# Five small moves of work at stage ends in a two-block transformer kernel: down-projection inputs, selected rows, a key product's bank, low parts

## The reference

```python
q = (xc @ wq).reshape(PEER_CHUNK, PEER_HEADS, 2, half)
sc = jnp.einsum('chpd,hpnd->chpn', q, sub_keys)
s1, i1 = lax.top_k(sc[:, :, 0], PEER_TOPK)          # 16 of 128 in each half
s2, i2 = lax.top_k(sc[:, :, 1], PEER_TOPK)
# the best 16 of the 16 x 16 sums, softmax g over them, expert index = i1 * 128 + i2
a = gelu(einsum('chkd,cd->chk', u[eidx], xc), exact)
out = einsum('chk,chkd->cd', g * a, v[eidx])
```

```python
hn = rmsnorm(h, norm_ffn_pre)
g, up = jnp.split(hn @ w_gate_up, 2, axis=-1)       # 2816 each
h = h + rmsnorm((jax.nn.silu(g) * up) @ w_down, norm_ffn_post)
```

## Time and profile before

| what | us |
|---|---|
| median of 3 runs | 2596.41 |
| lowest and highest | 2592.62, 2598.65 |
| profiled execution, its own time | 2602.34 |
| span of the profiled execution | 2600.5 |
| TensorE busy | 2461.7 (95%) |
| VectorE busy | 1758.9 (68%) |
| ScalarE busy | 1339.2 (51%) |
| GpSimd busy | 700.6 (27%) |

### The profile page before, as it was taken

How to read it: one execution, slowest core, us unless ns; L and a number is a source line. 1 busy time by engine, 2 the same in 40 slices (tenths; PEclk the granted TensorE clock), 3 DMA queues, 4 the chain that set the end, 5 groups by cost and what they waited for, 6 DMA issues and landing times. The chain is left out here.

```text
span 2600.5 us, 57098 instructions
## 1 busy us (share of the span) xinstructions
PE 2461.7 (95%) x16535; PEld 2249.7 (87%) x16535; DVE 1758.9 (68%) x3854; ACT 1339.2 (51%) x2350; POOL 700.6 (27%) x533
## 2 busy tenths in 40 slices
PE   7889999999999999998899999999999989888998
PEld 6789999999888887888899999988888886778986
DVE  5637777887677777655777788777777665514346
ACT  3434555776555555443455577655555434323443
POOL 5655444000000000656444200000000150324665
PEclk9989999999999999999999999999999999888999
DMA  6234666445566666433466544456666544322543
GB/s 245 70 128 158 216 227 222 161 158 179 187 242 242 242 242 229 171 112 132 160 222 217 216 146 163 176 208 242 241 242 241 184 155 149 111 74 106 179 171 143
DMA packets 97759, 475.23 MB, mean 183 GB/s; under 512 B 11776, under 2 KB 13312, under 8 KB 50432
## 3 DMA queue, kind: packets, MB, share of 16 engines
q1 hardware_dynamic: 97104, 472.91, 50.6%
q10 hardware_dynamic: 560, 1.19, 0.1%
HBM read 438.41 MB, written 35.65 MB: 182 GB/s over the span
## 5 line engine op out<-in xcount | busy, mean ns | idle before, releaser
L1233 ACT ACTIVATE wh<-ring 128x512 fp32r<-128x512 f32 x1428 | 881.9, 627 | 618.6 <-ACTq L1232 616.0
L1758 DVE TENSOR_TENSOR wl<-ring,wh 128x512 fp32r<-128x512 f32 x961 | 683.7, 716 | 276.3 <-DVEq L1757 258.7
L485 POOL TENSOR_TENSOR wl<-ring,wh 128x512 fp32r<-128x512 f32 x295 | 389.7, 1341 | 1536.7 <-POOLq L484 1533.3
L972 PE MATMUL PS<-xh,wh 128*128 128x256 f32 x2048 | 593.9, 290 | 9.1 <-PEq L968 7.8
L972 PE MATMUL PS<-xl,wh 128*128 128x256 f32 x2048 | 579.2, 283 | 0.0
L972 PE MATMUL PS<-xh,wl 128*128 128x256 f32 x2048 | 579.2, 283 | 0.0
L798 PE MATMUL PS<-wh,xh 128*128 128x512 f32 x1112 | 435.1, 391 | 7.3 <-PEq L795 7.3
L798 PE MATMUL PS<-wl,xh 128*128 128x512 f32 x1112 | 433.4, 390 | 0.0
L798 PE MATMUL PS<-wh,xl 128*128 128x512 f32 x1112 | 433.3, 390 | 0.0
L972 PEld LDWEIGHTS PS<-xh,wh 128*128 128x128 f32 x2048 | 391.9, 191 | 16.2 <-issue 15.4
L972 PEld LDWEIGHTS PS<-xl,wh 128*128 128x128 f32 x2048 | 392.4, 192 | 0.0
(11 more groups left out here) (292 smaller groups left out, 3750.9 us busy)
## 6 DMA issues: line engine op xcount, KB each, us to landing
ring<-in_peer_u SPq DMA_DIRECT2D x128, 1024.0 KB, 4.8
ring<-in_peer_v SPq DMA_DIRECT2D x128, 1024.0 KB, 4.8
acts<-stg SPq DMA_DIRECT2D x124, 256.0 KB, 2.0
gains<-acts SPq DMA_DIRECT2D x124, 256.0 KB, 4.8
ring<-in_w_in SPq DMA_DIRECT2D x24, 1024.0 KB, 4.9
ring<-in_w_gate_up SPq DMA_DIRECT2D x22, 1024.0 KB, 4.7
ring<-in_peer_wq SPq DMA_DIRECT2D x16, 1024.0 KB, 4.8
ring<-in_w_down SPq DMA_DIRECT2D x11, 1024.0 KB, 4.8
```

Source lines behind the costliest of these rows:

```text
L485: part = pool.tensor_tensor(wl[:, q, :], ring[:, s, q * QW:(q + 1) * QW], wh[:, q, :].bitcast(F32), SUB)
L972: last = pe.matmul(PS[:, 2 * j, 0:S], w[:, q, k * P:(k + 1) * P], x[:, at, :], start=at + i == 0, stop=at + i == 9)
L1233: act.activation(wh[:, q, :], ring[:, s, q * QW:(q + 1) * QW], ACT.Copy).then_inc(high_ready[q], 1)
L1758: part = dve.tensor_tensor(wl[:, q, :], ring[:, s, q * QW:(q + 1) * QW], wh[:, q, :].bitcast(F32), SUB)
```

## The change

- The last two gate-up chunks are taken out of the loops of TensorE and DVE. In the last one, TensorE signals a new semaphore `x_used` with the first product of quarter 1. DVE waits for it and stages both halves of the first down chunk before it takes the last gate-up result. ACT casts quarters 0 to 2 of the first down chunk before the last silu and quarter 3 after it.
- The transposes of the selected rows stand before chunk 37 of the experts, not behind it. DVE copies them before the low part of quarter 3 of chunk 38.
- The last key product of a layer writes bank 4 (slot 2) and waits for that slot.
- In `residual_rows` the low part of the next chunk's quarter 3 stands between the two sums of squares.

```diff
-            def chunks(n, first, f, full, scales=None):
+            def chunks(n, first, f, full, scales=None, x_done=None):
...
-                with pe.Fori(0, n // 2 - 1):
+                with pe.Fori(0, n // 2 - (2 if x_done else 1)):
                     for s in (0, 1):
                         f(s, full)
+                if x_done:
+                    f(0, full)
+                    f(1, full, x_done)
...
+                                if x_done and q == 1 and b + k + i == 0:
+                                    last.then_inc(x_done, 1)
...
-                def key_scores(c, s):
-
-                    pe.wait_ge(slot_free[1], 1)
-                    pe.sem_inc(slot_free[1], -1)
+                def key_scores(c, s, slot=1):
+
+                    pe.wait_ge(slot_free[slot], 1)
+                    pe.sem_inc(slot_free[slot], -1)
...
-                key_scores(N_WQ - 1, 1)
+                key_scores(N_WQ - 1, 1, 2)
...
-                with pe.Fori(0, N_GATE):
+                with pe.Fori(0, N_GATE - 1):
                     experts()
...
                                [(ps2(2 + t)[:, i * P:(i + 1) * P], sel[:, i, t, :]) for i in range(3)])
+                experts()
...
-            chunks(NFB, first_cols, chunk_by_cols, dve_full, row_scales)
+            chunks(NFB, first_cols, chunk_by_cols, dve_full, row_scales, x_used)
...
+                if next_first:
+                    for q in range(3):
+                        high(n % 2, q)
                 if result:
                     result(n - 1, (n - 1) % 2)
+                if next_first:
+                    high(n % 2, 3)
...
                 def scores_out(c, s):
 
-                    act.wait_ge(act_full[1], 1)
-                    act.sem_inc(act_full[1], -1)
+                    slot = 2 if isinstance(c, int) and c == N_WQ - 1 else 1
+                    act.wait_ge(act_full[slot], 1)
+                    act.sem_inc(act_full[slot], -1)
...
-            high_parts(NFB, squares_to_xT, silu, peel=1)
-            high_parts(NFB // 2)
+            high_parts(NFB, squares_to_xT, silu, peel=1, next_first=True)
+            high_parts(NFB // 2, begun=True)
...
                     s, cols = c % 2, slice(CW * c, CW * (c + 1))
-                    if c:
-                        low(s, 3)
                     take_rows(s)
...
                     for t in range(TT):
                         sum_of_squares(o_all[:, t, cols], t, sums4[:, t, c:c + 1])
+                        if t == 0 and c < 3:
+                            low(1 - s, 3)
...
-                for q in range(4):
+                for q in range(3):
                     low(0, q, 2)
                 for t in range(TT):
                     dve.wait_ge(dve_full[2 + t], 1)
...
+                low(0, 3, 2)
                 own(dve.engine_nop())
...
+            with dve.Fori(1, NFB // 2 - 1) as i:
+                for s in (0, 1):
+                    low(s, 3)
+                    gate_up(s, 2 * i + s)
+            low(0, 3)
+            gate_up(0, NFB - 2)
+            low(1, 3)
+            dve.wait_ge(x_used, 1)
+            dve.sem_inc(x_used, -1)
             for j in range(2):
                 stage_down(0, j)
+            gate_up(1, NFB - 1)
+
             low(0, 3)
```

More of the change, by code:

```diff
@@ L207, in build @@
         acc_seen = sem("acc_seen")
+        x_used = sem("x_used")
         dve_lows_done = sem("dve_lows_done")
@@ L763, in rows_by_chunk, with chunk_by_cols @@
                     last.then_inc(full[s], 1)
-            def chunk_by_cols(s, full):
+            def chunk_by_cols(s, full, x_done=None):
                 pe.wait_ge(slot_free[s], 1)
@@ L936, in _ @@
                 pe.wait_ge(keys_in, 16)
-                def key_scores(c, s):
-                    pe.wait_ge(slot_free[1], 1)
-                    pe.sem_inc(slot_free[1], -1)
+                def key_scores(c, s, slot=1):
+                    pe.wait_ge(slot_free[slot], 1)
+                    pe.sem_inc(slot_free[slot], -1)
                     for t in range(TT):
                         for p in range(2):
-                            last = pe.matmul(PS[:, 2, (2 * t + p) * NK:(2 * t + p + 1) * NK],
+                            last = pe.matmul(PS[:, 2 * slot, (2 * t + p) * NK:(2 * t + p + 1) * NK],
                                              qTc[:, s, p, t * P:(t + 1) * P],
                                              peer_k[:, c, p * NK:(p + 1) * NK], start=True, stop=True)
-                    last.then_inc(act_full[1], 1)
+                    last.then_inc(act_full[slot], 1)
                 first_cols(act_full)
@@ L1235, in high_parts @@
             def high_parts(n, between=None, result=None, peel=0, late=None, following=False,
-                           mid=None, begun=False):
+                           mid=None, begun=False, next_first=False):
                 if not begun:
@@ L1403, in scores_out @@
                 def scores_out(c, s):
-                    act.wait_ge(act_full[1], 1)
-                    act.sem_inc(act_full[1], -1)
+                    slot = 2 if isinstance(c, int) and c == N_WQ - 1 else 1
+                    act.wait_ge(act_full[slot], 1)
+                    act.sem_inc(act_full[slot], -1)
                     act.wait_ge(scores_used, 1)
                     act.sem_inc(scores_used, -1)
-                    act.activation(scc[s][:, :, :], PS[:, 2, :].rearrange("p (a n) -> p a n", a=4),
+                    act.activation(scc[s][:, :, :], PS[:, 2 * slot, :].rearrange("p (a n) -> p a n", a=4),
                                    ACT.Copy).then_inc(act_own, 1)
@@ L1412, in scores_out @@
                     act.sem_inc(act_own, -1)
-                    act.sem_inc(slot_free[1], 1)
+                    act.sem_inc(slot_free[slot], 1)
                     act.sem_inc(scores_ready, 1)
@@ L2522, in gate_up @@
                 dve.sem_inc(act_used, 1)
[L2524 to L2530, removed]
             def stage_down(c, j):
@@ L2537, in stage_down @@
                                   SUB).then_inc(wst_ready[j], 1)
+            gate_up(0, 0)
+            low(1, 3)
+            gate_up(1, 1)
+            with dve.Fori(1, NFB // 2 - 1) as i:
[4 more added lines that the diff above has]
+            gate_up(0, NFB - 2)
+            low(1, 3)
+            dve.wait_ge(x_used, 1)
+            dve.sem_inc(x_used, -1)
             for j in range(2):
                 stage_down(0, j)
+            gate_up(1, NFB - 1)
             low(0, 3)
```

## The result

The changed kernel takes 2583.18 us in the median of five runs (2578.61 to 2585.24); the kernel before took 2596.41 us beside it (2592.62 to 2604.5). The ratio is 0.994, with a 95% interval of 0.9925 to 0.9956. The forecast was 2584 us. The profiled execution took 2583.18 us, with a span of 2581.4 and a mean granted clock of 0.982 (before 2602.34, 2600.5 and 0.975). The profiles are 19.1 us apart and the medians 13.2, and the interval of the ratio reaches from 11.4 to 19.5 us. Of the profiles' 19.1 us, 4.1 lie in a place that nobody touched: it is told at the end.

What follows compares the result with a forecast made beforehand. TensorE, busy 95% of 2600.5 us, was taken to bound the kernel, so only its waits and the slow clock behind them could be won. 6.5 + 4.1 + 1.6 + 0.3 = 12.5 us off the median 2596.41 gave about 2584, range 2577 to 2592.

Steps and rivals of the forecast that it cites:

- down parts early: End of gate-up: 5.15 us wait and 1.9 us of clock go, 0.55 comes back; 6.5 us, between 5.0 and 7.0.
- low parts between sums: Output stages: waits of 2.28 and 0.53 us go, with 1.3 of slow clock; 4.1 us, between 2.0 and 4.6.
- transposes sooner: Before the one-hots: they start sooner, 0.8 us a layer, TensorE still waiting 2 us; 1.6 us, between 0.4 and 2.2.
- own bank: Last key product: its 2.67 us wait goes, but TensorE waits later for DVE; 0.3 us for both layers.
- middle case for DVE: Early down staging: first cast and subtraction go through, POOL holds the second pair, TensorE waits 0.35 us; 6.5 us gained.
- giving back: Down stage: 0.55 us returned, 0.35 for a late fourth low part and 0.2 for the third chunk's late ring half.
- Rival (a): Key product: DVE is no barrier, all 5.3 us come in place of 0.3; 2573 to 2580 us, chance 0.12.
- (b): Routing loops: the first layer takes on the second's waits, 6.1 us against 0.3, costing 5.8; 2590 us, chance 0.13.
- (c): Routing loops: a 1.7 us wait more in each of 16 turns, so slower; 2611 us, chance 0.04.
- sign of trouble: Routing loops: the prediction is wrong if waits in the two together change by more than 5 us.
- (d): Down stage: staging held four times and ring late, only half of 6.5 us won; 2587 us, chance 0.08.
- (e): All edited places: the change doesn't remove what it aims at, no measurable change; 2594 us, chance 0.06.

Runs made afterwards that it cites:

- stage_early: The changed kernel, but ACT casts all four quarters of the first down chunk after the last silu, as before; 2584.21 us, ratio 0.9943.
- cast_early: The changed kernel, but DVE stages the first down inputs after the last gate-up result, as before; 2586.57 us, ratio 0.9947.
- scores_first: The changed kernel, with ACT copying the seventh pair's scores out before the four casts of the first expert chunk; 2581.01 us, ratio 0.994.
- onehots_first: The changed kernel, with the first one-hot group built before the low part of chunk 38's fourth quarter; 2578.7 us, ratio 0.9924.
- both_first: The changed kernel with the edits of scores_first and onehots_first together; 2582.71 us, ratio 0.9932.
- copies_first: onehots_first, with DVE's two copies of the selected rows also ahead of the low parts of quarters 1 and 2; 2580.17 us, ratio 0.9921.
- row_only: The kernel before with only the selected rows transposed one chunk sooner; 2596.08 us, ratio 0.9988.
- low_only: The kernel before with only the low part moved between the two sums of squares; 2590.93 us, ratio 0.9966.
- key_only: The kernel before with only the last key product in its own bank; 2598.38 us, ratio 1.0002.
- down_only: The kernel before with only the down-stage part of the change; 2595.87 us, ratio 0.9978.
- after_again: The changed kernel unaltered, run again beside its variants; 2582.13 us, ratio 0.994.

## Why the prediction was right

| term | predicted | in the trace | run again |
|---|---|---|---|
| down parts early | 6.5 (5.0 to 7.0) | 5.4; alone 4.8 | 5.3 |
| low parts between sums | 4.1 (2.0 to 4.6) | 5.3 to 5.7; alone 5.3 | 5.3 |
| transposes sooner | 1.6 (0.4 to 2.2) | 2.0 | 0.5 |
| own bank | 0.3 (0 to 0.35 per layer) | 0.7 | 0.7 |
| sum | 12.5 | 13.4 to 13.8 | 11.8 |
| medians | 12.4 | 13.2 | |
| ratio as a time | | 15.6 (11.4 to 19.5) | 15.6 (11.4 to 19.5) |

**Down: the mechanism right, the term too large.** The first wait, the steps after it and the request of the third chunk (2509.06; 2522.7 less the 13.4 gained earlier is 2509.3) behaved as worked out. ACT's and POOL's early parts and DVE's staging are both needed, which stage_early and cast_early show. The middle case for DVE came true: first pair free, second held. The step that failed is the giving back. The sum took off 0.35 us for a late fourth low part and 0.2 for the third chunk's ring half, 0.55 in all; the waits behind the first product grew by 1.25. The two named are small or absent here (0.19 and 0.28 us at the second and third chunk), but a wait of 1.25 us stands in the fourth, where DVE's staging for it and POOL's low parts start within 0.3 us of each other. The same kernel run again has it (1.2), and scores_first, onehots_first, both_first and copies_first have 1.2, 1.2, 1.2 and 1.5. A kernel with the down part alone has one of 1.4, but ahead of the second chunk, also behind a cast and a subtraction of DVE that were held beside POOL's low parts. Of the two with half of the part, stage_early has 0.6 in the fourth chunk and cast_early 0.5 and 0.6 in the fifth and sixth, and the kernels without the part (before, row_only, low_only, key_only) have none over 0.35 behind the first wait. So it belongs to the early start. That the DVE operations beside POOL's are its cause is read from their rows; no kernel moved them apart. I had followed the change only as far as the third chunk. The clock gave 1.5 us instead of 1.9, since the first down chunk takes 5.85 us without its waits and not 5.55.

This agrees with the rule of the Trainium skill, page "SBUF — State Buffer", section "Who interferes with whom", that such operations of VectorE and GpSimd hold each other for a whole instruction and that the first to issue goes ahead: 0.42 us against 1.29 for one subtraction, 0.69 against 1.33 and 1.69 for one low part. The rule leaves it to the order of issue, and that changed from one execution to the next (the second cast above, 0.29 and 1.40).

**Low parts: the mechanism right, the term too small.** The second stage gave 4.0 us where 2.28 + 1.3 = 3.6 were expected, since the clock gave back some 1.5 to 1.7 instead of 1.3. The first stage was priced at its one wait of 0.53; it gave 1.3 or a little more, in steps of 0.7, 0.3 and 0.4 at waits of 0.53, 0.10 and 0.19. The last two are small waits at other quarters of that stage which the row I chose did not show. The one of 0.19 stands in row_only, key_only and down_only too and belongs to the edit; the one of 0.10 is absent in them, so that step is variation, and some 1.1 us are the edit's.

**Transposes: right up to the first one-hot product, and then left open.** The wait fell by 0.5 us, to 2.32 instead of the 2.0 expected, but the transposes also filled a wait ahead of them, and both together gave 1.0 us per layer instead of 0.8. This much recurs in both layers of all six traces with this part and a wait of 2.3 us. The prediction put the clock behind the wait that stays at nothing, and this was right in only one of six traces for the first layer: in the other five it took 1.55 us back. In the second layer the traces with this part gain 1.0 or 2.5 us, but key_only and low_only gain 1.6 without it and down_only loses 1.2. What this part is worth in a median stays open: the two layers gave 2.0 us in one execution of the changed kernel and 0.5 in the next, and row_only's interval reaches from -0.3 to 6.2.

**Own bank: right in kind.** TensorE waits later instead, 0.83 + 1.09 = 1.9 us where 2.5 were named. The low part of the fourth quarter took 0.69 instead of 1.03 us, and the quarter starts 0.34 us sooner, which is the upper end of what was given for a layer, and it came in both layers. Rival (a), which had 5.3 us here, is excluded by key_only (0.7 us in its trace) and scores_first.

**The routing loops, rivals (b) and (c).** TensorE's waits in the expert chunks of the first layer (245 to 470) and of the second (1262 to 1480), in this order for before, changed, down_only and low_only:

```profile
PE PS L972 <- PEq L968: 1.1, 4, 0.3
...
PE PS L972 <- PEq L968: 6.4, 11, 1.7
```

```profile
PE PS L978 <- PEq L974: 1.8, 5, 0.5
...
PE PS L978 <- PEq L974: 2.9, 6, 1.4
```

```profile
PE PS L978 <- PEq L974: 3.1, 11, 0.4
...
PE PS L978 <- PEq L974: 3.3, 6, 1.7
```

```profile
PE PS L972 <- PEq L968: 2.1, 7, 0.5
...
PE PS L972 <- PEq L968: 1.0, 3, 0.5
```

down_only and low_only run the program of before up to the end of the second layer, and yet their second layer waits 3.1 and 5.4 us less and their first 2.0 and 1.0 more. The difference between the layers that I read into rival (b) is variation between executions of one program. The changed kernel's sum went from 7.5 to 4.7 us, under the 5 us that I had named as the sign of trouble, and no run had a wait there longer than 1.7. Rivals (b) and (c) did not come true, and one profile of before could not have priced (b). Rivals (d) and (e) are excluded by the first down product without a wait and by the ratio's upper end of 0.9956.

The prediction subtracted its terms from the median rather than from the profiled execution's own time, which stood 5.9 us above it. That choice mattered more than any term but the first. It was argued for, but how near 2584 came to 2583.18 is partly luck: the kernel before had a median of 2599.3 in 35 later runs, and 2599.3 less 12.5 is 2586.8. By the ratios the change is worth some 15.6 us in both series, more than the 11.8 or 13.8 that its places gave in the traces. The rest is not shown; the untouched stretch of the last section could hold it, for which the prediction had no term.

## What to carry to other kernels

When a wait is held by two chains on different engines, both must be moved: here either half alone left 3.4 or 3.9 of 5.15 us, and at the key product moving the one not yet moved only brought the other forward. When a stage starts earlier, follow the next chunks until the order of the engines that hold each other up has settled, not one or two of them: the price of the early start stood in the fourth chunk in six traces and in the second in one. Behind a wait of 2.3 us that is left in place, look at the clock as well: it made the difference between 1.0 us won and 0.5 lost in one layer. A gain of a few us in a kernel whose runs spread over 10 is better read from the starts of one engine's instructions laid side by side than from a dozen timings, and what two executions of the same stretch of program differ by is to be known before such a difference is explained.

## What the runs showed of the hardware

**The clock in an untouched stretch.** Between the two output stages lies the cross attention, which the change does not touch. The stretch of its 112 products, by engine, in before, in the changed kernel and in the changed kernel run again (the first column is the stretch, the second its length, and the clock is the third from the end):

```profile
2306.00:2343.00 37.00, 29.00 (x112) 24.21 (x112) 5.72 (x8) 7.99 (x14) 3.71 (x3) 0.72 0.00 0
```

```profile
2299.40:2332.60 33.20, 24.89 (x112) 21.24 (x112) 5.76 (x9) 7.98 (x14) 3.72 (x3) 0.84 0.01 2
```

```profile
2296.90:2334.20 37.30, 29.04 (x112) 24.25 (x112) 5.76 (x9) 7.98 (x14) 3.72 (x3) 0.72 0.00 1
```

The changed kernel ran more of this stretch at 2.4 GHz and gained 4.1 us there (its starts go from -6.5 to -10.6), with the same waits of TensorE inside it. The same kernel run again does not have these 4 us, so the program alone does not decide it. But it is not plain luck either: of the eight traces of kernels with the whole change or nearly all of it, seven have the short form (after_again has the long one), and of the five of before and the single parts none has it. Whether the change makes the short form more frequent, and what decides it, stays open.

**One operation, two durations.** Besides the low parts and the staging, the eight sums of squares of the changed kernel's second output stage took 1.40, 1.06, 0.56, 0.42, 1.07, 1.35, 0.56 and 0.41 us, and copies_first has the same to 0.02. The six over 0.5 started while POOL made low parts, the two of 0.56 near the end of one; the other two started while POOL stood still.
